# A decoder trunk on one core: the last taps of the second half's long convolution computed on ScalarE and GpSimd

## The reference, cut to what matters

```python
h = rms_norm(x, norm1_g) * (1 + sc1) + sh1            # x: 2048 tokens of 1024
proj = h @ w_in                                       # 1024 -> 2304
qa, ka, va, ub, uc, ud = split(proj)
ya = diff_attention(qa, ka, va, ...)                  # 4 heads, two causal softmax maps each, 128 queries a block
yb = conformer_conv(ub, ...)                          # below
yc = bg * causal_dwconv(cg * xc, short_conv_w)        # 3 taps
yd = multiscale_pool(ud, pool_w, pool_scale)          # windows 2, 4, 8, 16, then a 64x64 product per group
x = x + g1 * (concat(ya, yb, yc, yd) @ w_out)
h = rms_norm(x, norm2_g) * (1 + sc2) + sh2
x = x + g2 * (square(relu(h @ w_ff1)) @ w_ff2)

def conformer_conv(u, dw_w, dw_b, ln_g, ln_b):
    val, gate = split(u)
    h = causal_dwconv(val * sigmoid(gate), dw_w) + dw_b   # 31 taps per channel, 256 channels
    return silu(layer_norm(h, ln_g, ln_b))
```

## Time and profile before

| | us |
|---|---|
| median of 3 runs (lowest to highest) | 2452.62 (2447.08 to 2458.55) |
| the profiled execution, its own time | 2452.15 |
| its span in the trace | 2450.4 |
| busy: TensorE products / VectorE / ScalarE / GpSimd | 2330.2 / 1768.1 / 965.2 / 318.3 |

### The profile page before, as it was taken

The page is one execution under the profiler, slowest core; times in us unless marked ns, Lnnn a source line. Parts: engine busy times, 40 slices in busy tenths (PEclk is TensorE's granted clock), DMA queues, the critical chain, the costliest instruction groups (busy, mean ns, idle before and its releaser), DMA issues.

```text
span 2450.4 us, 31254 instructions
## 1 busy us (share of the span) xinstructions
PE 2330.2 (95%) x11634; PEld 1961.5 (80%) x11634; DVE 1768.1 (72%) x2666; ACT 965.2 (39%) x1577; POOL 318.3 (13%) x219
## 2 busy tenths in 40 slices
PE   6999999977889898999999999999999999999999
PEld 3988797756879887878888888888878888888887
DVE  2648796888889776687767676767687666666666
ACT  2632454247888763422323232323433232323231
POOL 0343043322344440000000000000000000000000
PEclk8999999977999889999999999999999999999999
DMA  5442334120000024111111111126111111111112
GB/s 211 158 150 78 122 129 155 48 95 26 14 10 27 10 95 130 43 35 52 52 51 51 51 51 51 51 75 223 55 51 52 50 53 50 52 51 52 51 51 86
DMA packets 107735, 177.67 MB, mean 73 GB/s; under 512 B 5480, under 2 KB 77436, under 8 KB 106620
## 3 DMA queue, kind: packets, MB, share of 16 engines
q1 hardware_dynamic: 107644, 176.45, 21.9%
HBM read 152.84 MB, written 23.59 MB: 72 GB/s over the span
## 4 chain that ended last, share of the span: by engine, by line
PE 79%; DVE 11%; DMA 3%; ACT 3%; issue 2%; POOL 1%; SPq 1%; DVEq 0%; ACTq 0%; POOLq 0%
PE ps L2324 9%; PE ps L2325 9%; PE ps L2326 9%; PE ps L2361 7%; PE ps L2362 7%; PE ps L2363 7%; PE ps L2032 4%; PE ps L2034 4%; PE ps L2033 4%; PE ps L2215 3%; DVE ps L1488 3%; PE ps L2200 3%; PE ps L2235 2%; PE ps L2270 2%; PE ps L2272 2%
## 5 line engine op out<-in xcount | busy, mean ns | idle before, releaser
L1840 DVE TENSOR_TENSOR sb_x_new<-sb_x_new,ps 128x512 f32<-128x512 f32 x512 | 347.9, 685 | 110.9 <-PE ps L2326 105.3
L2324 PE MATMUL ps<-sb_w_hi,sb_u_hi 128*128 128x512 f32 x1024 | 400.8, 391 | 11.3 <-DVE sb_x_new L1840 11.3
L2325 PE MATMUL ps<-sb_w_lo,sb_u_hi 128*128 128x512 f32 x1024 | 400.4, 391 | 0.0
L2326 PE MATMUL ps<-sb_w_hi,sb_u_lo 128*128 128x512 f32 x1024 | 400.0, 391 | 0.0
L2324 PEld LDWEIGHTS ps<-sb_w_hi,sb_u_hi 128*128 128x128 f32 x1024 | 193.5, 189 | 52.5 <-DVE sb_x_new L1840 12.2
L2326 PEld LDWEIGHTS ps<-sb_w_hi,sb_u_lo 128*128 128x128 f32 x1024 | 193.5, 189 | 40.4
L2325 PEld LDWEIGHTS ps<-sb_w_lo,sb_u_hi 128*128 128x128 f32 x1024 | 193.6, 189 | 40.2
L2034 PE MATMUL ps<-sb_h_hi,sb_w_lo 128*128 128x512 f32 x512 | 199.4, 389 | 0.0
L2032 PE MATMUL ps<-sb_h_hi,sb_w_hi 128*128 128x512 f32 x448 | 178.4, 398 | 0.8 <-DVE sb_w_lo L1802 0.7
L1334 ACT ACTIVATE ps<-ps 128x512 f32<-128x512 f32 x28 | 16.3, 582 | 410.8 <-PE ps L2363 410.8
L2033 PE MATMUL ps<-sb_h_lo,sb_w_hi 128*128 128x512 f32 x448 | 174.4, 389 | 0.0
(11 more groups left out here) (259 smaller groups left out, 4955.2 us busy)
## 6 DMA issues: line engine op xcount, KB each, us to landing
sb_w_full<-in_w_ff SPq DMA_DIRECT2D x34, 1024.0 KB, 5.1
sb_w_full<-in_w_ff SPq DMA_DIRECT2D x56, 512.0 KB, 3.8
sb_w_raw<-in_w_in SPq DMA_DIRECT2D x18, 1024.0 KB, 5.5
sb_ada<-in_w_ada SPq DMA_DIRECT2D x32, 512.0 KB, 6.0
sb_ada_first<-in_w_ada SPq DMA_DIRECT2D x8, 1024.0 KB, 7.5
sb_x_in<-in_x SPq DMA_DIRECT2D x16, 512.0 KB, 5.5
sb_mix_in<-mix_scratch SPq DMA_DIRECT2D x16, 512.0 KB, 4.7
sb_x_new<-in_x SPq DMA_DIRECT2D x16, 512.0 KB, 4.9
```

The lines of the kernel that those rows point to most:

```text
L1840: V.tensor_tensor(out=y, in0=y, in1=psum[:, 4 + p % 4, :], op=ALU.add).then_inc(ff2_read, 1)
L2324: M(dst, uh, wh[:, j, col], start=j == order[0], stop=False, skip_group_check=fast)
L2325: M(dst, uh, wl[:, j, col], start=False, stop=False, skip_group_check=fast)
L2326: ins = M(dst, ul, wh[:, j, col], start=False, stop=j == order[1], skip_group_check=fast)
```

## The change

In the second half the last 6 taps of block 0 and the last 10 taps of block 1 (`SHARED`) leave VectorE. ScalarE multiplies: the first of these taps goes straight into `acc` (`begin_sum`), the others into a ring of four tiles `tap` (`make_taps`), and GpSimd adds them to `acc` one by one (`add_taps`), 10 for block 0 and 18 for block 1. VectorE ends each block with two additions of its PSUM banks to `acc`, which also give the signal `conv_moved`; the two `move_conv` of the second half are gone. GpSimd's additions stand in its stream behind all window sums; after the third addition of block 1 it waits until VectorE has read the norm vector. SP waits for all 28 additions before it loads v, since `tap` lies in `v_sb`'s place. `read_norm_vector` moves behind the small copy into `prod` (in both halves). Attention steps 0 to 2 take what is left of the taps (4 each before), and `LN_STEP` becomes 6.

```diff
+SHARED = (6, 10)
+def shared_taps(b):
+    return [(j, cc) for j in range(TAPS - SHARED[b], TAPS) for cc in range(GC)]
+SHARED_NO = [0, len(shared_taps(0)) - GC, len(shared_taps(0)) + len(shared_taps(1)) - 2 * GC]
-LN_STEP = 14
+LN_STEP = 6
+        tap = [sb(f"tap{s}", 162.5 + 2 * s, [P, BLK]) for s in range(4)]
...
 (SP)
+            sp.wait_ge(tap_added, SHARED_NO[2])
             sp.dma_start(v_sb[:, :, :], qkv_v[:, :, 2 * GW:3 * GW]).then_inc(v_ld, 16)
...
 (GpSimd)
+            def add_taps(b, first, last):
+                for n in range(first, last):
+                    j, cc = shared_taps(b)[GC + n]
+                    n += SHARED_NO[b]
+                    pool.wait_ge(tap_ready, n + 1)
+                    pool.wait_ge(tap_first, GC * (b + 1))
+                    if n >= GC:
+                        pool.wait_ge(tap_added, n - GC + 1)
+                    y = acc[:, cc, b * BLK:(b + 1) * BLK]
+                    pool.tensor_tensor(out=y, in0=y, in1=tap[n % 4][:, :], op=ALU.add).then_inc(tap_added, 1)
...
                     if h and b == 0:
                         ln_out(0, 1)
+            add_taps(0, 0, SHARED_NO[1])
+            add_taps(1, 0, 3)
+            pool.wait_ge(norm_read, 2)
+            add_taps(1, 3, SHARED_NO[2] - SHARED_NO[1])
...
 (ScalarE)
+            def begin_sum(b):
+                act.wait_ge(conf_ready, NB * GC + GC * (b + 1))
+                act.wait_ge(ln_st[b], 16)
+                for j, cc in shared_taps(b)[:GC]:
+                    A(acc[:, cc, b * BLK:(b + 1) * BLK], conf[:, cc, b * BLK + j:b * BLK + j + BLK], ACT.Copy,
+                      scale=col2[:, R_DWW + GC * j + cc:R_DWW + GC * j + cc + 1]).then_inc(tap_first, 1)
+            def make_taps(b, first, last):
+                for n in range(first, last):
+                    j, cc = shared_taps(b)[GC + n]
+                    n += SHARED_NO[b]
+                    if n >= 4:
+                        act.wait_ge(tap_added, n - 3)
+                    A(tap[n % 4][:, :], conf[:, cc, b * BLK + j:b * BLK + j + BLK], ACT.Copy,
+                      scale=col2[:, R_DWW + GC * j + cc:R_DWW + GC * j + cc + 1]).then_inc(tap_ready, 1)
...
                 A(stage[n % 2][:, :], bank(o), ACT.Copy, scale=col1[:, R_PSC + cc:R_PSC + cc + 1]).then_inc(poolout_ready, 1)
+                if n >= NB * GC:
+                    last = SHARED_NO[2] - SHARED_NO[1] + n - 2 * NB * GC
+                    make_taps(1, last, last + 1)
...
                 w_in_head(w0 + 6)
+                if h:
+                    begin_sum(0)
+                    make_taps(0, 0, 4)
...
-                move_conv(h, 0)
+                    move_conv(0, 0)
+                else:
+                    make_taps(0, 4, SHARED_NO[1])
+                    begin_sum(1)
+                    make_taps(1, 0, SHARED_NO[2] - SHARED_NO[1] - 4)
                 each_block("pool", h, to_pool_stage)
...
-                if u == 13:
-                    move_conv(1, 1)
...
 (VectorE)
-                    for j in range(TAPS):
+                    taps = TAPS - (SHARED[b] if h else 0)
+                    for j in range(taps):
...
+                    if h:
+                        dve.wait_ge(tap_added, SHARED_NO[b + 1])
+                        for cc in range(GC):
+                            y = acc[:, cc, b * BLK:(b + 1) * BLK]
+                            dve.wait_ge(dve_chain, marks[cc - GC])
+                            ins = V.tensor_tensor(out=y, in0=conv_bank(cc), in1=y, op=ALU.add)
+                        ins.then_inc(conv_moved, 1)
...
                 pump(taps, 20)
-                read_norm_vector(h)
                 if h:
                     dve.wait_ge(lnout_ready, NB * GC)
                 link(V.tensor_copy(prod[:, :, 0:STAPS - 1], halo2[:, :, :]))
+                read_norm_vector(h)
...
-                pump(taps, 4 if u < 12 else 9 * TAPS)
+                pump(taps, 4 if u < 3 else 9 * TAPS)
```

More of the change, by code:

```diff
@@ L340, in trunk @@
         ff2_mm, ff2_read, out_st = [sem(n) for n in ("ff2_mm", "ff2_read", "out_st")]
+        tap_first, tap_ready, tap_added = sem("tap_first"), sem("tap_ready"), sem("tap_added")
         wo_part, gate_st, gate_ld = sem("wo_part"), sem("gate_st"), sem("gate_ld")
@@ L997, in qk_root @@
                 A(small[:, 48:64], small[:, 32:48], ACT.Sqrt, bias=eps_col, scale=1.0 / QKD).then_inc(qrms_ready, 1)
+            def begin_sum(b):
[12 more added lines that the diff above has]
+                      scale=col2[:, R_DWW + GC * j + cc:R_DWW + GC * j + cc + 1]).then_inc(tap_ready, 1)
             def move_conv(h, b):
                 act.wait_ge(conv_ready, NB * h + b + 1)
-                if h:
-                    act.wait_ge(ln_st[b], 16)
                 for cc in range(GC):
@@ L1488, in conv_taps @@
                                 ins = V.scalar_tensor_tensor(out=dst, in0=src, scalar=w, in1=dst, op0=ALU.mult, op1=ALU.add)
-                            if j == TAPS - 1 and cc == GC - 1:
+                            if h == 0 and j == taps - 1 and cc == GC - 1:
                                 ins.then_inc(conv_ready, 1)
```

## The result

The changed kernel takes 2436.02 us (median of 8 runs, 2431.81 to 2439.41), the kernel before beside it 2446.99 (8 runs, 2441.48 to 2458.55). The ratio is 0.9944, with a 95% interval of 0.9928 to 0.9959: 0.56% faster, some 13.7 us (10 to 18); the two medians themselves lie 11.0 us apart. Two later series gave ratios of 0.9943 and 0.9946. The prediction was 2441, in a range of 2435 to 2450, with "within 0.5%" as the likeliest class. The time fell inside the range, but that class did not come: by the ratio the gain is just beyond the 12.3 us that are 0.5%, and the interval reaches to either side of them. The predicted gain of 11.4 us is 2 to 3 short of 13.7. The forecast time is 5 us too long, also because the 2452.62 us that it started from lie above every other median of the kernel before (2446.99 to 2451.4).

What follows compares the result with a forecast made beforehand. VectorE was taken to bound the kernel from 456 us, by its taps, and attention's steps until unit 11. Attention -14.0 and the stretch before +2.6 gave -11.4 from 2452.15: 2440.8, plus 0.5 for the median, 2441; range 2435 to 2450.

Steps and rivals of the forecast that it cites:

- within 0.5%: Whole kernel: class for changes under 12.3 us, given 0.52, against 0.42 for faster and 0.06 for slower.
- Layer norm: Attention, layer norm moved from step 14 to 6: same work, 1.5 us lost, bounds 0 and 4.
- the two sums: Layer norm's sums on TensorE, 1.94 us each at full clock: at the lower clock 1.4 us more each.
- ScalarE's wait: Layer norm, ScalarE waiting for `ln_scale`: the 3.01 us wait stays.
- Hold of the last pooling operations: Last `pooled` on VectorE, held by GpSimd's first additions: the 20 taps start 2.2 us late, bounds 0 and 4.5.
- Additions at 1.24 us: GpSimd's 28 additions of 128x512: 1.24 us each; forecast wrong if they take over 1.5.
- three held operations: Earlier VectorE operations meeting GpSimd's, 2.28, 2.79 and 1.15 us long, read as agreeing with the skill's rule of mutual exclusion.
- Clock at the mean: TensorE at the pooling's mean, waiting 2 us longer at 490: clock can stay low longer, 0.4 us lost (0 to 1.4).
- Taps off the attention steps: Attention units 4 to 10: 14.5 us gained from ScalarE's waits, 1.0 more from `move_conv(1, 1)`, together 15.5.
- TensorE as the bound of the steps: Rival, attention steps 4 to 10: clock stays at 0.50, 3.3 us a step, -3.7 us in all, 2449; chance 0.20.
- The pause: GpSimd's wait for the norm vector's read: keeps nothing apart, as three additions end before it; counted at nothing.
- -14.0 + 2.6: Whole kernel: 14.0 us gained in attention, 2.6 lost in the stretch to the mean (bounds 0 and 6).

Runs made afterwards that it cites:

- ln14: Changed kernel with the last block's layer norm put back to attention's step 14, taps still moved: 2439.58 us, 3.7 more than the changed kernel beside it.
- s66: Changed kernel with six shared taps a channel in the second block instead of ten, eight taps back on VectorE in attention's steps 3 and 4: 2439.39 us.
- held: Changed kernel with all of GpSimd's additions kept back until VectorE's last pooling operation and its copy are done: 2434.87 us.
- noadds: Changed kernel with GpSimd's 28 additions left out of the computation: 2428.99 us, 7 below the changed kernel.
- base: The kernel before, unchanged, run once more for a second trace: 2447.73 us in a single execution.
- late6: Changed kernel with six VectorE taps moved behind the last of the four products with the gate and the gate row's read: 2431.01 us against 2436.99.

## Where the prediction held, and the step that failed

- **Layer norm.** The step that failed, and with it the call "within 0.5%": 1.5 us lost was predicted (0 to 4), 3.7 gained was measured (`ln14`). The prediction priced the two sums at the lower clock and ScalarE's wait, and took the gap as equal at both places, which it nearly is; the extra price around the layer norm itself came out at 0 to 1.2 us. It left out what stands behind the gap: there steps of 640 keys wait for TensorE at the lower clock and those of 384 don't (ScalarE's waits for the transposes 7.9 us against 1.7), though it had cited the clock of 0.64 from 605 to 610. That is 2.7 us in the trace of `ln14`, and between nothing and 2.0 in the two of the kernel before; where the rest of the 3.7 lies stays open.
- **Hold of the last pooling operations.** Predicted 2.2 us, measured 2.23 net (459.56 - 453.73 against 456.30 - 452.70). Additions at 1.24 us, no wait of VectorE at block 0's sums, the last `in_prod` done at 490.5 net (490.4 predicted), all additions done at 495.3 net (494.6): as worked out. One of the three held operations that the prediction reads as agreeing is a copy with a single SBUF input, which its sentence on two inputs doesn't cover.
- **Clock at the mean.** Mis-sized: 0.4 us was taken (0 to 1.4), 1.0 came between the two traces shown (3.25 less 2.23). VectorE's wait for the mean is 4.52 us in two traces of the changed kernel and 3.29 in the third, 3.57 and 1.88 in the two of the kernel before. So the change added between nothing and 2.6 us, by the execution, and the 1.0 is one draw.
- **Taps off the attention steps.** Mis-sized: 15.5 us predicted. With the layer norm left at step 14 the trace's difference to before goes from +3.0 at unit 3 to -10.8 at unit 15, 13.8 gained. At units 4 to 10 of `ln14` 2.3 us of ScalarE's waits stay, which the steps without taps were taken not to have; `s66` shows the same from the other side, 0.4 us a tap instead of 0.66.
- **TensorE as the bound of the steps** (rival): falls. With TensorE busy for all of 540 to 545 us the clock rose from 0.51 there to 1.00 from 545 to 550.
- **The pause.** The prediction held that it keeps nothing apart, having looked at additions 10 to 12 only. It went wrong in what stands behind the pause: without it 24 additions ran in one go, and the copy or, with the copy moved, the first of the vector's two small operations was held not for one addition but for the rest of that run. Without the pause the change gives 1 to 4 us instead of 13.
- **The class.** -14.0 + 2.6 was -11.4; the runs give 11 to 14. Taps and clock at the mean were put too favourably by some 2 us and the layer norm too dear by 5, two errors of opposite sign, so that the sum came out nearer than its terms by luck. The sum lay 0.9 us from the threshold, so its sign of error decided the class; the bounds of the layer norm's term (0 to 4 lost) excluded a gain for no reason in the rows.

What is not settled: why some executions without the pause (three of twelve) escape the hold, since no trace of one was taken; and which events move the lead by 0.8 to 2.3 us at units 20 to 25, 41 and 54 in kernels that differ only far ahead, or not at all. What moving the norm vector behind the copy is worth was not measured by itself.

## What to carry to other kernels

Price a serial step that empties TensorE by what runs behind it too: the gap cost about the same at both places here, the low clock after it only where the steps then waited for TensorE. Take two traces of a kernel before a clock's price is put down to a change: here the same kernel had it in one and not in the other. Before moving work to GpSimd list every small VectorE operation from SBUF to SBUF that falls into its run, however few elements it has, and break the run there. And move filler work behind the last producer that another engine waits for, not ahead of it.

## What the runs showed of the hardware

- A VectorE copy of 128x4 elements lasted 11.59 us and an operation on 128x8 elements 7.87 us, each to the end of a run of GpSimd additions of 1.24 to 1.26 us; taps into PSUM, products from PSUM and a reduction kept 0.66, 0.69 and 1.22 us beside such runs.
- GpSimd's additions were slowed where VectorE got its turn between them: 13 took 17.20 us around the last pooling operations, 16.31 when all were kept behind these (`held`), and 14 took 17.33 later.
- TensorE worked without a break from 470 to 485 us and then stood idle ahead of the last pooling product. In the three traces of the changed kernel, idle for 3.42 us, the granted clock fell towards its lower level of 1.2 GHz (0.53 to 0.79 in the stretch at the mean) and the mean took 3.62, 3.62 and 2.40 us; in the first trace of the kernel before, idle for 2.96, it took 3.53. Idle for 2.19 (`noadds`), 2.09 (`base`) or 0.71 us (`late6`), the clock stayed at 2.4 GHz and the mean took 1.88.
